# Hybrid decoder trunk on one core: the linear recurrence's decay levels joined into two products of 192 queries, its vector work re-timed, and the start, the key slabs and the end re-ordered

## The reference, cut to what matters

```
h = rms_norm(x, pre_norm)                       # x: (256, 1024)
z = h @ w_in                                    # 1024 x 12848, one combined projection
q, kc, vc, ks, vs, kw, vw, gate, silu_a, v_b, silu_b, q_c, f_c, i_c, silu_c, merge = split(z)
o_a = nsa_mixer(...) * silu(silu_a)             # compressed blocks, selected blocks, window
o_b = pool_mixer(v_b) * silu(silu_b)            # causal means over 2, 4, 8, 16 tokens
o_c = rms_norm(hgrn2_mixer(q_c, f_c, i_c)) * silu(silu_c)
merged = sum over branches of sigmoid(merge) * (branch @ w_branch)
x + rms_norm(merged @ w_out, post_norm)
```

```
# hgrn2: 8 heads of 128 channels
f = lb + (1 - lb) * sigmoid(f_logits);  k = 1 - f;  A = cumsum(log f)
o[t] = sum over s <= t of (sum_d q[t,d] k[s,d] exp(A[t,d] - A[s,d])) v[s]
# compression: blocks of 32 positions, stride 16 (15 blocks), 4 groups
ck[c] = sum_p (kc[16c + p] + pe_k[p]) @ w_ck[p];   cv[c] the same with vc, pe_v, w_cv
```

## Time and profile before

| | |
|---|---|
| three runs, median | 486.56 us (486.48 to 486.65) |
| the profiled execution's own time | 485.57 us |
| its span, first to last instruction | 483.8 us |
| PE busy | 475.2 us (98%) |
| DVE busy | 343.2 us (71%) |
| ACT busy | 264.6 us (55%) |
| POOL busy | 159.1 us (33%) |
| mean DMA rate | 158 GB/s |

### The profile page before, as it was taken

One profiled execution on the slowest core, in us unless ns is written; L12 is line 12 of the kernel. 1 busy time (PEld: TensorE's weight loads), 2 busy tenths in 40 slices (PEclk: granted clock), 3 DMA queues, 4 the chain that ended last, 5 costly groups with the idle time before them and its releaser, 6 DMA issues.

```text
span 483.8 us, 9621 instructions
## 1 busy us (share of the span) xinstructions
PE 475.2 (98%) x3948; PEld 463.9 (96%) x3948; DVE 343.2 (71%) x577; ACT 264.6 (55%) x398; POOL 159.1 (33%) x157
## 2 busy tenths in 40 slices
PE   9999999999999999899999999999999999999995
PEld 8999999999999999889999999999999999999995
DVE  4898967798976566797896747878584257655653
ACT  6887744594562737553565346576554245433531
POOL 1074820807100009990256415436745120000000
PEclk9999999999999999999999999999999999999999
DMA  8956634454354755555355343253525536677502
GB/s 297 330 170 192 189 103 143 125 171 142 119 175 122 188 137 166 155 164 184 119 187 162 106 133 113 87 156 107 174 89 173 175 120 192 213 233 246 175 1 87
DMA packets 76006, 76.43 MB, mean 158 GB/s; under 512 B 5759, under 2 KB 74751, under 8 KB 75963
## 3 DMA queue, kind: packets, MB, share of 16 engines
q1 hardware_dynamic: 75675, 75.64, 50.4%
q10 hardware_dynamic: 288, 0.18, 0.2%
HBM read 74.77 MB, written 1.05 MB: 157 GB/s over the span
## 4 chain that ended last, share of the span: by engine, by line
PE 94%; DVE 2%; ACT 2%; issue 1%; DVEq 0%; ACTq 0%
PE ps L997 75%; PE ps L1022 4%; PE ps L1160 3%; PE ps L1111 2%; PE ps L1185 1%; PE ps L1100 1%; PE ps L1179 1%; PE ps L1127 1%; DVE WL L629 1%; PE ps L1023 1%; PE ps L1114 1%; PE ps L1038 1%; PE ps L1129 1%; PE ps L1128 1%; PE ps L1065 1%
## 5 line engine op out<-in xcount | busy, mean ns | idle before, releaser
L997 PE MATMUL ps<-hH,WL 128*128 128x256 f32 x688 | 195.6, 288 | 1.2 <-DVE WL L629 1.2
L997 PE MATMUL ps<-hL,WH 128*128 128x256 f32 x688 | 194.8, 284 | 0.0
L997 PE MATMUL ps<-hH,WH 128*128 128x256 f32 x688 | 194.8, 284 | 0.0
L629 DVE TENSOR_TENSOR WL<-W,WH 128x2048 fp32r<-128x2048 f32 (+1 forms) x66 | 152.9, 2317 | 19.5 <-PE ps L997 17.1
L432 ACT ACTIVATE WH<-W 128x2048 fp32r<-128x2048 f32 (+1 forms) x66 | 124.7, 1889 | 47.9 <-PE ps L997 46.6
L997 PEld LDWEIGHTS ps<-hH,WL 128*128 128x128 f32 x688 | 130.6, 191 | 2.3 <-DVE WL L629 1.4
L997 PEld LDWEIGHTS ps<-hL,WH 128*128 128x128 f32 x688 | 131.8, 192 | 0.8 <-issue 0.7
L997 PEld LDWEIGHTS ps<-hH,WH 128*128 128x128 f32 x688 | 131.7, 191 | 0.0
L394 POOL TENSOR_SCALAR R<-R,st 128x256 f32<-128x256 f32 x32 | 29.2, 924 | 82.1 <-DVE st L804 82.1
L997 PE MATMUL ps<-bH,WL 128*128 128x256 f32 x192 | 54.9, 286 | 0.0
L997 PE MATMUL ps<-bH,WH 128*128 128x256 f32 x192 | 54.3, 283 | 0.0
(11 more groups left out here) (192 smaller groups left out, 779.3 us busy)
## 6 DMA issues: line engine op xcount, KB each, us to landing
W<-w_in SPq DMA_DIRECT2D x48, 1024.0 KB, 5.2
W<-w_branch SPq DMA_DIRECT2D x12, 1024.0 KB, 5.3
W<-w_out SPq DMA_DIRECT2D x4, 1024.0 KB, 5.4
W<-w_in SPq DMA_DIRECT2D x2, 608.0 KB, 3.8
R<-x SPq DMA_DIRECT2D x2, 512.0 KB, 4.6
W<-w_in SPq DMA_DIRECT2D x2, 512.0 KB, 6.7
R<-cmp_w SPq DMA_DIRECT2D x2, 512.0 KB, 8.5
OC<-pool_w SPq DMA_DIRECT2D x4, 256.0 KB, 5.9
```

The costliest lines, as they stand in the source:

```text
L629: dve.tensor_tensor(slab_view(WL[:, s % 2], s), slab_view(W[:, s % 3], s), slab_view(WH[:, s % 3], s), ALU.subtract).then_inc(s_lo, 1)
L997: mm = pe.matmul(o, l, r, start=(at == 0 if mixed else k0 + k == 0 and j == 0), stop=(at == len(order) - 1 if mixed else k0 + k == KC - 1 ...
```

## The change

The diff has six parts.

1. Recurrence, products: the levels of 32 and 16, and of 8 and 4, are joined. With a block width b of 16 (then 4), four blocks form a group, and a query block refers to the last position of each earlier key block of its group: three pairs at distance 1, two at distance 2, one at distance 3 (`STEPS`), so that 64 queries make 96 columns and 128 queries 192. A unit is then two products of 192 columns, one of 64 (width 64), one of 128 and, for the second half, another of 128. POOL, ACT and DVE compute exponents, exponentials and products for these, and DVE collects six predicated pieces of 96, 64 and 32 elements and one plain copy of 64x64.
2. Recurrence, order: scans at s = 2, 5, 6, 8; the query multiplications at `MUL_AT`, ahead of the low weights of the step; root and normalisation at `RSTD_AT` and `NORM_AT`. POOL's second pair waits for the first multiplication.
3. Slab order: the compression's slabs come first after the recurrence's, the keys at 24 and 25, the last query slab at 26.
4. Compression: ACT copies the blocks (8 copies of 64x240 for each slab); the position vectors ride as a 61st column, which DVE writes with four small copies at the start, and are added after the product. DVE does this, and copies the value blocks, at s = 27.
5. Around the key slabs DVE forms `lo(s + 2)` ahead of `read(s)`.
6. Start: ACT's two DMA issues (identity, small vectors) go to SP behind x; DVE sums half of the second tile's squares; the scaling is split between DVE and ACT; ACT's copy of the first half slab is cut in two, the second piece behind `hH`'s second tile. End: the first three partial sums are added early and enter the root as its bias.

```diff
-LEVELS = (128, 64, 32, 16, 8, 4)
+RADIX = (16, 4)
+STEPS = ((0, 3, 1), (3, 2, 2), (5, 1, 3))
...
+    out += [("kc", 0, "in", C_KC), ("vc", 0, "in", C_VC), q[2], ("vs", 0, "in", C_VS)]
+    out += [("vwk", 0, "in", C_VW), ("vw", 0, "in", C_VW)]
+    out += bv[0:2] + q[0:2] + bv[2:4] + [("ks", 0, "in", C_KS), ("kw", 0, "in", C_KW), q[3]]
...
-SCAN_AT = (2, 6, 10, 14)
+SCAN_AT = (2, 5, 6, 8)
+MUL_AT = (7, 10, 11, 14, 15, 18, 19, 22)
+RSTD_AT = (15, 19, 22, 26)
+NORM_AT = (16, 20, 23, 27)
...
+                if p == 1:
+                    pool.wait_ge(s_hmul, 1)
...
+            act.activation(WH[:, 0, 0:2, :], W[:, 0, 0:2, :], ACT.Copy).then_inc(s_hi0a, 1)
+            act.wait_ge(s_small, 16)
             for c in range(KC):
+                if c == 2:
+                    act.activation(WH[:, 0, 2:FIRST_A, :], W[:, 0, 2:FIRST_A, :], ACT.Copy).then_inc(s_hi0a, 1)
                 act.wait_ge(s_xt, c // 2 + 1)
...
+            for j in range(2):
+                dve.wait_ge(s_hi0a, j + 1)
+                dve.tensor_tensor(WL[:, 0, 2 * j:2 * j + 2, :], W[:, 0, 2 * j:2 * j + 2, :],
+                                  WH[:, 0, 2 * j:2 * j + 2, :], ALU.subtract).then_inc(s_lo0, 1)
             dve.wait_ge(s_land[0], 16)
             dve.tensor_copy(WH[:, 0, FIRST_A:KC, :], W[:, 0, FIRST_A:KC, :]).then_inc(s_hi0b, 1)
...
                 early(s)
-                if mixing(s - 1):
+                multiply(s)
+                if mixing(s - 1) and SLABS[s][0] != "kw":
                     lo(s + 1)
                 mix(s)
+                keys = SLABS[s][0] in ("ks", "kw")
+                if keys:
+                    lo(s + 2)
                 read(s)
...
-                for lv in range(1, NLV):
-                    b = LEVELS[lv]
-                    t = q[:, lv, hp, P * i:P * i + P]
-                    up = t.rearrange("p (n w) -> p n w", w=2 * b)[:, :, b:2 * b]
-                    pe.matmul(ps[:, b0, 64 * (lv - 1):64 * lv], t, up, start=(lv == 1), stop=False)
+                for r in range(2):
+                    pe.matmul(ps[:, b0, 192 * r:192 * r + 192], OWN[e][r][:, hp, t],
+                              REACH[e][r][:, hp, 192 * i:192 * i + 192], start=(r == 0), stop=False)
```

More of the change, by code:

```diff
@@ L22 @@
 NCMP = (T - CB) // CS + 1
+CROWS = GROUPS * NCMP + 1
 SCALE = HEAD ** -0.5
@@ L1213, in constant_table @@
     s = np.arange(P)[:, None]
-    j = np.arange(64)[None, :]
-    for n, b in enumerate(LEVELS[1:]):
-        t = (j // b) * 2 * b + b + j % b
-        k[:, K_MASK + 64 * n:K_MASK + 64 * n + 64] = (s // (2 * b) == t // (2 * b)) & (s % (2 * b) < b)
+    j = np.arange(192)
+    for n, b in enumerate(RADIX):
+        step = j // b % 6
+        far = np.array([1, 1, 1, 2, 2, 3])[step]
+        key = 4 * (j // (6 * b)) + np.array([0, 1, 2, 0, 1, 0])[step]
+        assert (far + key % 4 < 4).all()
+        k[:, K_MASK + 192 * n:K_MASK + 192 * n + 192] = s // b == key[None, :]
     t = np.arange(P)[None, :]
```

284 lines of the change are left out of this document (165 added, 119 removed).

## The result

The changed kernel has a median of 490.93 us over 22 runs (484.55 to 493.47), the kernel before 485.99 over 22 (485.14 to 486.85). The ratio is 1.0047, 95% interval 1.0025 to 1.0068. Forecast were 481.2 us and a range of 479.4 to 484.3: the sign and the range both missed. The changed kernel's times stand at three levels, 484.6 to 485.1 (6 runs), 490.7 to 491.6 (7) and 492.3 to 493.5 (9), with a mean granted TensorE clock of 0.997 to 1.0, 0.983 to 0.986 and 0.979 to 0.983; those of before stand at two, 485.1 to 485.5 and 486.5 to 486.9. The ratio leaves out the changed kernel's highest level. What parts the levels turns out to be the cause of most of the loss.

A forecast was written before the change was run, and what follows sets the result against it. PE, busy 98% of the span, was taken to bound the kernel, plus its few late starts. Terms -3.8 - 2.5 + 0.7 + 0.3 - 0.1 = -5.4 us took the median 486.56 to 481.2 us, range 479.4 to 484.3.

The forecast's parts named there:

- PE's passes in the units: Recurrence units: 192-column passes at 0.164 us each cut a unit from 1.12 to 0.88; 16 units, 3.8 us less.
- rivals by columns: Units: passes are paid for by columns, so 3.5 us more in place of 3.8 less; 488.5 us, chance 1%.
- VectorE crowded in every step: Steps 10 to 22: POOL crowds DVE's multiplications, PE waits 1.8 in each of seven steps; 494 us, chance 4%.
- Start: Start through slab 5: later low weights and DVE work cost 0.7 us more, between 0.3 less and 1.6 more.
- The 0.65 for product 0: First slab's product: PE waits at `hL` and low weights, so product 0 ends 0.65 us later.
- ACT at 55% hides them: Compression's reads moved to ACT: 3.2 us twice off DVE, hidden by an ACT that is 55% busy.
- Forecast for step 15/16: DVE after a query slab's read: starts 1.4 late at step 15, yet 0.1 us counted as spare.
- The term that holds this step: DVE and POOL in the units: thin spares cost 0.3 us more, between 0 and 3.
- 2.5 us less: PE's late starts at slab 28 and the value blocks, 1.37 and 1.11 us, vanish by queue order; between 0 and 2.5.
- rival (e): Late starts only move to other steps, where another read ends last; 483.7 us, chance 5%.
- No part of the sum is a matter of clock: Whole kernel: granted clock 9 in all 40 slices, its upper level of 2.4 GHz, so clock adds nothing.
- the end itself: Kernel's end: DVE's sum of 0.16 leaves the path; 0.1 us less, 0 to 0.2.

The follow-up runs named there:

- the nine profiles named above: Profiles of kernels with the changed order of loads and no edit to the start; the first product ended anywhere from 15.83 to 17.43 us.
- the stop given to the kernel before: Kernel before plus 1.8 to 2.0 us of unused-buffer fills on VectorE ahead of slab 31's low weights; four runs: 487.59, 487.77, 493.55, 494.10 us.

## Why the prediction was wrong

- **PE's passes in the units: right.** 3.8 less forecast, 16 times 0.24 to 0.25, so 3.9, measured, 192 columns at 0.162. The rivals by columns, and of VectorE crowded in every step, did not come about.
- **Start: 0.7 forecast, 1.12 by slab 5, within the bound of 1.6.** The 0.65 for product 0 was 0.20 in this profile, but that is luck: over the nine profiles named above product 0 ended on average at 16.55, for 16.7 forecast. I took the transposes' start at 8.18 as fixed. It is not: the passes on zeros start 0.21 us apart at first and 0.11 apart from some moment on, which was 7.3 us in the profile of before, 5.1 in this one and between 4.5 and 7.3 in all fourteen, so that here the transposes began at 7.13. Where the zeros end early, scaling x sooner does buy something: with the start of before and zeros that ended 0.6 sooner the 16 transposes took 2.20 us instead of 1.91 (the profile of the stop given to the kernel before). The wait ahead of slab 3's low weights did absorb a part, as forecast: these began 0.55 late (23.34 for 22.79). But slab 5's began 1.55 late (37.23 for 35.68). The 1.0 between is VectorE's own: its forget-gate operations took longer while POOL was writing exponents in its new order, for instance two of 1.22 and 1.41 us that had taken 0.74 and 0.78.
- **"ACT at 55% hides them": the step that failed first.** The copies were priced on VectorE, from where they left, and not on ScalarE, where they arrive. No ScalarE operation of that form was in the trace, so bounds were due, and the copies had to be put in ScalarE's queue ahead of the exponential and of q's copies. Forecast for step 15/16: 0.1 us of spare. Step 16 stood in the list of what would show the prediction wrong. Measured: a stop of 2.45 us, of which changing only the order in which the copies walk took away 2.29. The term that holds this step, 0.3 us more, had bounds of 0 to 3; the 2.45 lies within them, but it was priced for VectorE's small spares and not for ScalarE's queue. With the copies back on VectorE the gain was 1.65, so hiding them was not free there either.
- **"2.5 us less" for the two late starts: wrong in what it is worth.** Both causes were named rightly, and both waits left their places. But VectorE runs from 202.96 to 221.16 almost without a gap, and slab 31 waits for the end of that: of 2.12 us won up to slab 30, 1.71 were given back at slab 31. That is rival (e), to which I gave 5%. Its price of 2.5 us back was near, its chance far too low: I looked for what is late next only one or two steps ahead. Nor did I see that the change puts 1.21 us of `CKS` subtractions into that run of work. One edit, low weights 28 into an idle stretch of VectorE, did pay 2.07.
- **"No part of the sum is a matter of clock": the costliest sentence.** One profile at full clock was taken for a property of the kernel. The runs of before stood at two levels, and the late starts of the earlier trace rows already drop the clock in some executions. The change gathered late starts into a stop right ahead of the one product that has small matmuls inside, where a fall costs 5.9 to 6.3 us. That the stop brings the fall is shown: filling it removes the upper levels in all ten runs, and giving the kernel before a stop there brings such a level in two of four. Why some executions fall and others do not stays open.
- **The sum** by the profiled execution: units -3.8, start +1.1, slab 16 +2.45, late starts -0.4, clock +6.3, drifts and end -0.4: +5.3, the difference of the spans; the end itself is 0.16 shorter, for 0.1 forecast. Without the clock the change is worth 0.7 us by the middles of the lower levels (484.7 against 485.4) and 1.0 by this sum.

## What to carry to other kernels

Price a moved operation on the engine that takes it, in the shape of its write as well as its read, and follow that engine's queue until something that TensorE needs. When a wait is removed, follow the late engine's chain to the next point where it has slack; if there is none, the wait only moves, and it may merge with others into a longer stop. A TensorE stop of one or two microseconds is not worth just its length: look at what stands behind it, compare several runs' times for levels before believing a clock row, and where the stop can't go, fill it.

## What the runs showed of the hardware that was not expected

- Behind stops of 1.1 to 2.5 us TensorE's clock fell from 2.4 to 1.2 GHz for a while, in some executions and not in others of the same kernel. The price in profiled runs was 1.5 us with ordinary products behind (slab 16, 3.30 to 4.84; slab 29, 5.74 to 7.22; 3.4 us at half clock) and 5.9 with small matmuls among them (slab 31, 9.1 to 15.0; 13.7 us at half clock).
- At the start TensorE's passes of 128 columns on zeros halved their distance, from 0.21 to 0.11 us, at a moment between 4.5 and 7.3 us that differed from run to run.
- ScalarE's copy of 64x240 float32: 625 ns with writes 61 elements apart, 366 to 374 dense; the read's stride in PSUM (2 or 16) made 8 ns. VectorE's took 405 in its order.
- TensorE's pairs of float32 passes of 61 and 64 columns start 0.058 us apart with neighbouring elements and 0.11 with elements 16 apart.
- In the eleven profiles in which slab 0's first half was the fifth request of the queue, ScalarE began to copy it anywhere from 7.64 us, without a wait, to 9.65, after a wait of 1.82 for its landing. In that last run product 0 ended 1.19 us later than in the changed kernel's profile, and slab 5 started 1.22 later.
- VectorE's operations took longer at times when POOL worked: in the changed kernel slab 29's low weights 3.12 us for 2.28.
